# Product of the second expert table with its weights stationary, 32 tokens of it gathered instead, and the last gate computed with tokens along the free axis

## What is computed

```python
def peer(xn, w_pq, sub_k1, sub_k2, expert_u, expert_v):
    # 8 heads: top 16 of 128 keys on either side, top 16 of their 256 sums: 128 experts of 16384 a token
    act = jax.nn.gelu(jnp.einsum('tkd,td->tk', expert_u[ib], xb))
    return jnp.einsum('tk,tkd->td', act * gb, expert_v[ib])

h = h + peer(rms_norm_2(h, ffn_norm_gain), w_pq, sub_k1, sub_k2, expert_u, expert_v)
gate = jax.nn.sigmoid(rms_norm_2(h, ple_norm_gain) @ w_ple_gate)
h = h + gate * (p @ w_ple_proj)
```

## Time and profile before

| | us |
|---|---|
| median of 3 runs (3193.03 to 3201.77) | 3196.07 |
| the profiled execution, its own time | 3203.04 |
| its span | 3201.3 |
| PE busy | 3064.3 |
| DVE busy | 1886.7 |
| ACT busy | 1458.6 |
| granted clock of TensorE, mean share | 0.977 |

### The profile page before, as it was taken

One profiled execution on the slowest core, in us unless ns is written; L12 is line 12 of the kernel. 1 busy time (PEld: TensorE's weight loads), 2 busy tenths in 40 slices (PEclk: granted clock), 3 DMA queues, 4 the chain that ended last, 5 costly groups with the idle time before them and its releaser, 6 DMA issues. The chain is left out here.

```text
span 3201.3 us, 39991 instructions
## 1 busy us (share of the span) xinstructions
PE 3064.3 (96%) x15672; PEld 2653.1 (83%) x15672; DVE 1886.7 (59%) x2657; ACT 1458.6 (46%) x2137; POOL 159.9 (5%) x282
## 2 busy tenths in 40 slices
PE   8997689999998999999999999999999999999998
PEld 7996677888887887977789899889998888888876
DVE  4445355444444545464558987998755655655554
ACT  4333444444443444354444466347644444444443
POOL 2002100000000000140000100110000000000000
PEclk9996699999999999999999999999999999999999
DMA  7552045555554554545567888888787666777653
GB/s 247 188 188 68 0 148 172 192 185 194 185 188 158 192 196 145 173 142 178 192 211 247 281 304 305 293 278 294 257 276 241 240 231 242 242 248 248 216 194 131
DMA packets 219049, 665.24 MB, mean 208 GB/s; under 512 B 11705, under 2 KB 87513, under 8 KB 169488
## 3 DMA queue, kind: packets, MB, share of 16 engines
q1 hardware_dynamic: 208592, 607.36, 56.6%
q0 software_dynamic: 5440, 35.80, 3.2%
q10 hardware_dynamic: 4864, 19.99, 1.7%
HBM read 623.25 MB, written 37.77 MB: 206 GB/s over the span
## 5 line engine op out<-in xcount | busy, mean ns | idle before, releaser
L195 DVE TENSOR_TENSOR weights_lo<-weights,weights_hi 128x1024 fp32r<-128x1024 f32 (+4 forms) x1080 | 1227.5, 1178 | 974.8 <-ACT weights_hi L188 973.3
L188 ACT ACTIVATE weights_hi<-weights 128x1024 fp32r<-128x1024 f32 (+4 forms) x1080 | 1046.8, 1018 | 1508.8 <-PE banks L444 1121.4
L2185 PE MATMUL banks<-peer_features,weights_hi 128*128 128x448 f32 (+1 forms) x2304 | 743.7, 378 | 18.7 <-DVE weights_lo L195 18.6
L442 PE MATMUL banks<-weights_hi,features_hi 128*128 128x512 f32 (+3 forms) x1728 | 651.5, 377 | 11.4 <-DVE weights_lo L195 11.3
L444 PE MATMUL banks<-weights_hi,features_lo 128*128 128x512 f32 (+3 forms) x1728 | 649.3, 376 | 0.0
L443 PE MATMUL banks<-weights_lo,features_hi 128*128 128x512 f32 (+3 forms) x1728 | 649.1, 376 | 0.0
L2186 PE MATMUL banks<-peer_features,weights_lo 128*128 128x224 f32 (+1 forms) x2304 | 615.1, 267 | 0.0
L2185 PEld LDWEIGHTS banks<-peer_features,weights_hi 128*128 128x128 f32 x2304 | 431.9, 187 | 68.7 <-DVE weights_lo L195 27.9
L2186 PEld LDWEIGHTS banks<-peer_features,weights_lo 128*128 128x128 f32 x2304 | 438.6, 190 | 0.0
L442 PE MATMUL banks<-weights_hi,applied_hi 128*128 128x512 f32 x1024 | 398.5, 389 | 1.1 <-DVE peer_scores L2362 1.1
L444 PE MATMUL banks<-weights_hi,applied_lo 128*128 128x512 f32 x1024 | 398.4, 389 | 0.0
(11 more groups left out here) (377 smaller groups left out, 2101.8 us busy)
## 6 DMA issues: line engine op xcount, KB each, us to landing
weights<-in_expert_u SPq DMA_DIRECT2D x128, 1024.0 KB, 5.8
weights<-in_expert_v SPq DMA_DIRECT2D x128, 1024.0 KB, 5.0
weights<-in_w_ffn_gate SPq DMA_DIRECT2D x44, 1024.0 KB, 5.2
weights<-in_w_ffn_up SPq DMA_DIRECT2D x44, 1024.0 KB, 5.2
weights<-in_w_ffn_down SPq DMA_DIRECT2D x44, 1024.0 KB, 5.0
weights<-in_w_in SPq DMA_DIRECT2D x48, 900.0 KB, 4.7
weights<-in_w_out SPq DMA_DIRECT2D x32, 1024.0 KB, 5.2
weights<-in_w_in SPq DMA_DIRECT2D x24, 704.0 KB, 4.4
```

What stands on the lines that cost most here:

```text
L188: act.activation(hi[:, k, n], raw[:, k, n], ACT.Copy).then_inc(self.hi_ready, 1 + skip)
L195: last = dve.tensor_tensor(lo[:, k, n], raw[:, k, n], hi[:, k, n].bitcast(F32), ALU.subtract)
L442: pe.matmul(out, xh, wh, start=first, stop=False)
L2185: pe.matmul(self.bank(n % 3, 2 * (T - lo)), wh[:, k, :], F[:, k, :, lo:T], start=(k == 0), stop=False)
```

## The change

Five things are done.

1. **Table V turned.** The weights are stationary in chunks of 128 features, the gates of tokens 32 to 255 stream (224 columns): 16 chunks of three matmuls a piece. Of the three, the two with the rounded part of the weights come first (L2300, L2301), then lo weights (L2302). Two chunks share a bank; eight matmuls with a zero matrix (L2299) clear the banks first.
2. **V gathered for tokens 0 to 31.** POOL issues 32 more indirect DMAs, from the second table. DVE multiplies each with a weight and adds it to `row_sum`, in two halves (`ADD`, 64 instructions over steps 158 to 261). PE folds the sum in at e = 122 with 16 small matmuls (L2290). No one-hots and no stored scores for these tokens: buffers `S`, `a_hi`, `a_lo`, `s_in`, `g_in` lose 32 tokens.
3. **`SUM` moved.** The 64 half-row products of U stand at steps 56, 57, 58 to 73 and 108 to 153, one a step, none inside a retrieval step between 22 and 55 or 74 and 107.
4. **X transposed early.** At the eight steps 76, 79, ... 97 (`BACK`) PE transposes four blocks of X (L2263), and ACT copies them back, so that X has features on partitions.
5. **The gate continues the loop.** The pieces of w_ple_gate are steps 272 to 287 of the same block, weights stationary, 256 tokens streaming: 48 matmuls a piece. Adds, features, squares, and the result by groups of chunks are spread over the steps on ACT and DVE; the output is stored by features and turned on the host.

```diff
-        SC, RET, TURN = 18, (22, 74), (55, 107, 122)
-        HOT = [(58 + i, 0, ROWS // 8 + i) for i in range(16 - ROWS // 8)] + [(110 + i, 1, i) for i in range(16)]\
-            + [(126 + i, 0, i) for i in range(ROWS // 8)]
-        SUM = [34 + 4 * k // 3 for k in range(2 * ROWS)]
+        SC, RET, TURN = 18, (22, 74), (55, 107)
+        HOT = [(58 + i, 0, ROWS // 8 + i) for i in range(16 - ROWS // 8)] + [(110 + i, 1, i) for i in range(16)]
+        SUM = [56, 57, *range(58, 74), *range(108, 154)]
         DOTS = SUM[-1] + 1
+        free = [s for s in range(DOTS + 4, 262) if s % 8 != 2]
+        ADD = [free[k * len(free) // (2 * ROWS)] for k in range(2 * ROWS)]
+        GATHERED, BACK = NKEYS - 6, [76 + 3 * j for j in range(KD // 2)]
+        ROWSUM, SPREAD = 4, 6
...
-                    for c in range(ROWS):
+                    for c in range(2 * ROWS):
...
-                        pool.indirect_dma_start(out=rows[:, c % BUFS, :], out_offset=None, in_=rows_d,
-                                                in_offset=bass.IndirectOffsetOnAxis(ap=pick[:, c:c + 1], axis=0))\
+                        pool.indirect_dma_start(out=rows[:, c % BUFS, :], out_offset=None, in_=rows_d if c < ROWS else values_d,
+                                                in_offset=bass.IndirectOffsetOnAxis(ap=pick[:, c % ROWS:c % ROWS + 1], axis=0))\
...
-                        for t in ((1, 0) if e == 0 else (0, 1)):
-                            if e == 0 and t == 0:
-                                pe.wait_ge(tile_read, V0)
-                            for c in range(4):
-                                cols, tok = slice(c * BANK, (c + 1) * BANK), slice(t * P, (t + 1) * P)
-                                last = self.passes(pe, self.bank(4 * t + c), a_hi[:, q % 2, e % 2, tok], a_lo[:, q % 2, e % 2, tok],
-                                                   wh[:, cols], wl[:, cols], e == 0, e == NKEYS - 1)
+                        gh, gl = a_hi[:, q % 2, e % 2, :], a_lo[:, q % 2, e % 2, :]
+                        for c in (range(KD) if e > 0 else [*range(6, KD), *range(6)]):
+                            if e == 0 and c in (0, 2, 4):
+                                pe.wait_ge(tile_read, V0 - 2 + c // 2)
+                            out, cols = self.bank(c // 2, DENSE, c % 2 * T + ROWS), slice(c * P, (c + 1) * P)
+                            if e == 0 and c % 2 == 0:
+                                pe.matmul(self.bank(c // 2), zero[:, :], wh[:, 0:BANK], start=True, stop=False)
+                            pe.matmul(out, wh[:, cols], gh, start=False, stop=False)
+                            pe.matmul(out, wh[:, cols], gl, start=False, stop=False)
+                            last = pe.matmul(out, wl[:, cols], gh, start=False, stop=(e == NKEYS - 1 and c % 2 == 1))
...
+                    for s in range(KD):
+                        b, piece = s // 4, s % 4
+                        i, j, half = at(END + s)
+                        ring.wait(pe, i, j, half)
...
+                            for k in range(4):
+                                kk = 4 * piece + k
+                                if b == c == 0 and k % 2 == 0:
+                                    pe.wait_ge(*f_lo(kk // 2 + 1))
+                                out, cols = self.bank(4 * (b % 2) + c, T), slice(c * P, (c + 1) * P)
+                                pe.matmul(out, wh[:, k, cols], F[:, kk, 0, :], start=(kk == 0), stop=False)
+                                pe.matmul(out, wh[:, k, cols], F[:, kk, 1, :], start=False, stop=False)
+                                last = pe.matmul(out, wl[:, k, cols], F[:, kk, 0, :], start=False, stop=(kk == KD - 1))
...
+                            if c == 0:
+                                last = dve.tensor_scalar(to, row, weight, None, ALU.mult)
+                            else:
+                                last = dve.scalar_tensor_tensor(out=to, in0=row, scalar=weight, in1=to, op0=ALU.mult, op1=ALU.add)
...
+                    for s in range(KD):
+                        i, j, half = at(END + s)
+                        if s == 0:
+                            add(0)
+                            add(1)
...
+                        ring.split_lo(dve, ple_tiles, i, j, half)
+                        if s < 4:
+                            feature_lo(2 * s)
+                            feature_lo(2 * s + 1)
+                            if s < 3:
+                                add(2 * s + 2)
+                                add(2 * s + 3)
```

More of the change, by code:

```diff
@@ L1558, in project @@
             def project(pe, c, banks):
-                for t in range(NT):
+                for m in range(4):
                     for k in range(2):
-                        last = pe.matmul(self.bank(banks + t), pT[:, k, tok(t)], wproj[c // 2][:, c % 2, k, :],
-                                         start=(k == 0), stop=(k == 1))
+                        last = pe.matmul(self.bank(banks + m // 2, T, m % 2 * T), wproj[c // 2][:, c % 2, k, m * P:(m + 1) * P],
+                                         pT[:, k, :], start=(k == 0), stop=(k == 1))
                 last.then_inc(projected, 1)
@@ L2247, in _ @@
                                 last.then_inc(applied, 1)
                         last.then_inc(ring.used, 1)
+                    for s in range(KD):
+                        b, piece = s // 4, s % 4
+                        i, j, half = at(END + s)
+                        ring.wait(pe, i, j, half)
+                        wh, wl = [ring.piece(w, half, ple_tiles) for w in (ring.hi, ring.lo)]
+                        for c in range(4):
+                            if piece == 0 and b < 2:
+                                pe.wait_ge(added, 4 * b + c + 1)
+                            if piece == 0 and b >= 2:
+                                pe.wait_ge(gate_left, 2 * (b - 2) + c // 2 + 1)
+                            for k in range(4):
[6 more added lines that the diff above has]
+                                last = pe.matmul(out, wl[:, k, cols], F[:, kk, 0, :], start=False, stop=(kk == KD - 1))
+                            if b == 3 and piece == 3 and c < 3:
+                                last.then_inc(applied, 1)
+                        last.then_inc(ring.used, 1)
+                        if s == ROWSUM:
+                            pe.wait_ge(*x_squared(KD // 2 + 1))
+                            for t in range(NT):
+                                last = pe.matmul(self.bank(0, 1, T + t), total[:, 0, t * P:(t + 1) * P], self.ones[:, 0:1],
+                                                 start=True, stop=True)
+                            last.then_inc(self.squares.sem, 1)
+                        if s == SPREAD:
+                            pe.wait_ge(diag, 2)
+                            for t in range(NT):
+                                last = pe.matmul(self.bank(1, P, T + t * P), self.ones[:, :], diagonal[:, t * P:(t + 1) * P],
+                                                 start=True, stop=True)
+                            last.then_inc(spread, 1)
@@ L2400, in _ @@
                             dve.wait_ge(spread, 1)
-                            ch(dve.memset(S[:, :, :, 0:ROWS], 1.0))
+                            for quarter in range(4):
+                                ch(dve.tensor_copy(row_rstd[quarter * 32:quarter * 32 + 32, :], self.rstd[0:ROWS, 0:1]))
+                            dve.tensor_scalar(zero[:, :], self.ident[:, :], 0.0, None, ALU.mult)
+                            ch(dve.tensor_reduce(sel[:, :], self.ident[:, :].rearrange("p (q t) -> p t q", q=4), AX.X, ALU.add))
                         if s == 10:
@@ new lines, in feature_lo @@
+                    def feature_lo(j):
+                        dve.wait_ge(*f_hi(j + 1))
+                        for i in range(2):
+                            hi, lo = [f[:, 2 * j + i, :] for f in F_ple]
+                            last = dve.scalar_tensor_tensor(out=lo, in0=XT[:, j, i], scalar=ple_gains[2 * j + i],
+                                                            in1=hi.bitcast(F32), op0=ALU.mult, op1=ALU.subtract)
+                        last.then_inc(self.turned_read["dve"].sem, 1)
@@ L2463, in peer @@
+                    for n in range(6, len(groups)):
+                        scale(n)
+                        if n > 6:
+                            out(n - 1)
+                    out(len(groups) - 1)
             self.turn_split_close(gains)
```

334 lines of the change are left out of this document (214 added, 120 removed).

## The result

The changed kernel takes 3149.17 us (median of 4 runs, 3145.07 to 3151.32) against 3198.65 (4 runs): a ratio of 0.9846, 95% interval 0.9826 to 0.9865, so 49.5 us less. I had forecast 3130 with a range of 3095 to 3174. The direction and the range held; the gain is 49.5 us where my sum had 68.8. One sign that I had set myself did not hold: the second table was to be under 670 us, and it takes 692.8.

A forecast was written before the change was run, and what follows sets the result against it. PE was taken as busy nearly throughout, with DVE setting the pace in the first table's retrievals and two stretches without PE. The terms summed to -68.8 us, median 3127, stated as 3130 us, range 3095 to 3174.

The forecast's parts named there:

- Step 1: Second table: 6144 matmuls of 224 columns at 107 ns replace 3072 of 512, -39.0 us; added PE work +1.8 and +3.8.
- the first rival: Second table and gate: weight loads pace short matmuls, 113 ns apart, 37 and 5 us longer, total 3172; chance 0.15.
- the line: Matmul start distances, fitted through 512 and 352 columns: 0.419 ns a column and 12.2 ns beside them.
- Step 2: Second table: DVE's adds and POOL's gathers cost nothing, DVE's share going from 0.58 to about 0.76 under PE's cover.
- Step 3: First table's retrievals: half-row products moved out let pieces approach PE's 5.01 us, -23.0 us with a tenth left.
- Step 4: First table's one-hot steps: four go, each 1.85 us over a quiet piece, -7.4 us.
- Step 5: X turned early: 32 transposes of 0.12 us among PE's own work, +3.9 us; ACT's copies hidden.
- Step 6: Between second table and gate: the 10.2 us break goes but for 0.5 us, -9.7 us.
- Step 7: Gate: 768 matmuls of 256 columns replace 384 of 512, +5.9 us, or +10.5 with the pair's 126.5 ns.
- Step 8: Tail behind the last matmul: 14.3 us shrinks to 5.2, -9.1 us.
- Step 9: DMA in steps 126 to 153: gathers join weights, scores and gates at 337 to 350 GB/s, +4 us.
- DMA that can't follow: Gathers share engines with weights, scores and gates: at 290 GB/s +62 us, 3188; at 270 3243; chance 0.10.

The follow-up runs named there:

- e8_upair: Changed kernel with the first table's lo-weight matmul streaming 128 token columns instead of 224 in 14 of 16 chunks: 3144.82 us.
- e6_nogather: Changed kernel without the 32 gathers from the second table and DVE's waits for them, the adds kept: 3150.02 us.
- e5_sumback: Changed kernel with the first table's half-row products back at their old steps: 3168.81 us, ratio 0.9909 to the kernel before.
- e9_break: Changed kernel with all adds and features made in one block before the gate's first piece is split: 3156.50 us, ratio 0.9869 to the kernel before.
- e3_order: Changed kernel with the second table's three matmuls a chunk in the old order: 3151.19 us, ratio 0.9853 to the kernel before.
- e1_128: Changed kernel with the second table's matmuls streaming 128 token columns instead of 224: 3188.05 us, a single run.
- e2_half: Changed kernel with 64 of 128 stationary columns in the second table's matmuls, except in the first and last piece: 3095.75 us.
- e7_96x128: Changed kernel with 96 stationary columns and streams of 128 in the second table, except in the first and last piece: 3441.98 us, a single run.

## Why the prediction was right, and where it missed

- **Step 1, the distance in the second table, is the term that was mis-sized.** It had -39.0 for the matmuls alone; measured 6144 x 0.1117 = 686 against 696, -10. By my own signs, 0.112 and a second table of 670 us or more, the first rival is what happened. I had named this mechanism with 0.15 and nearly the right size, 113 ns, and set it aside by one argument: both pairs have 7 ns over the line, so the surcharge belongs to the pair. (Its 3172 was too high: it charged the gate 5 us that didn't come, and the other terms were better than my sum.) The argument doesn't hold. In the pair with 224 columns the load explains it (200 + 112 = 312, and e8_upair). For the pair with 256 it doesn't, since the gate's chain of 256 columns runs at the line's 120 ns; where those 7 ns come from stays open. The lower end, 0.10 us, was the distance between two starts, which is not the time that either takes. The chain of short matmuls that did stand in the trace, was the better witness. The formula that step 1 cites from the Trainium skill ("TensorE: Matmul & The Clock Gate", Back-to-back issue gap) is given there for a single matmul, not for a stream in which each brings its own weights.
- The zero products, +1.8: the first piece takes 7.21 us (2358.45 to 2365.66) against 5.36, +1.85. The fold-in, +3.8: its 32 records take 3.5 us, from 3014.22 to 3017.71. A term is missing behind it: the piece that follows takes 7.07 us instead of 5.36, +1.7, since the granted clock fell. In the window of the changed kernel right behind the fold-in PE is busy at 1.2 GHz:

```profile
3018.00:3021.00 3.00, 3.00 (x16) 3.00 (x15) 0.46 (x1) 0.00 (x0) 0.00 (x0) 0.50 0.65 208
```

- **Step 2**, gathers and adds in the second table hidden: right. DVE is busy 487 of 693 us, 0.70, where I had 0.76; e6_nogather shows no change.
- **Step 3**, -23.0: right, and the tenth that I left was not needed. 24 x 0.47 and 33 x 0.31 are 21.5 us with the transposes inside; without their 3.9 it is all of the 25.4. e5_sumback gives back 19.6 by the medians and 23.1 in the trace of the first table. The 23.1 with the transposes inside are 27 without them: pieces beside the 24 and 33 that I counted became faster too.
- **Step 4**, -7.4: the pieces from 126 to 129 lost their one-hots and went from 6.80 to 5.01 us, together 7.2. **Step 5**, +3.9: eight times four transposes; in pieces of 5.13 against 5.01 us it is 3.8.
- **Step 6**, -9.7, measured -10.1. e9_break shows that it is the order of DVE's work that does it.
- **Step 7**, +5.9, measured +6.3. The 256 columns are on the line.
- **Step 8**, -9.1, measured -9.8.
- **Step 9**, +4, measured 0: PE is never idle in the 80 us at 372 GB/s. I had taken 355 as the full rate from a share of 0.88; the trace goes beyond it.

The other rivals fell: the second of two matmuls with the same weights (e3_order), columns alone (e1_128), a stream on top of the load (0.112 is less than 0.18), retrievals that stay slow (5.01 us), and DMA that can't follow. No run points to a version that beats the changed kernel: 64 stationary columns free the stream but double the matmuls, and the rest of PE's time is full but for the 1.7 us that the clock costs behind the fold-in. A single matmul for both products with hi weights, writing twice to the same columns, wasn't tried on the chip.

## What to carry to other kernels

For fp32r matmuls that each bring their own 128 stationary columns, budget the larger of about 112 ns and the stream. By the line the two meet near 240 streamed columns (an estimate), and a shorter stream than that gains nothing. Look for a chain of short matmuls in the trace, however odd its line, before extrapolating from long ones, and read a chain by its period, never by one distance in a mixed pair. When several engines share steps, first ask whose queue sets the step: moving 64 products on DVE gave more here (about 20 us) than turning the matmuls of a 700 us stage (10). And look at the granted clock of a stage before you compare distances: at 1.2 GHz the same load took 213 ns.

## What the runs showed of the hardware

- The load of the stationary columns set the distance. At 2.4 GHz it was 111.7 ns for 128 columns whether 224 or 128 streamed, and 85 ns for 96. At 1.2 GHz it was 213 ns for 128 and 160 ns for 96. The Trainium skill ("TensorE: Matmul & The Clock Gate", LDWEIGHTS) gives columns / 1.2 in ns, 107 for 128 and 80 for 96; the traces agree within 5 ns at 2.4 GHz. At 1.2 GHz the runs show twice its figure.
- With 64 stationary columns a stream of 224 starts every 103 ns, 9.6 ns beside its columns at 2.4 GHz, where chains of 512 have 13.4.
- The granted clock fell to 1.2 GHz while PE was busy. In the changed kernel, e2_half, e5_sumback, e8_upair and e9_break it was 1.00 before the fold-in (32 records of 32 streamed columns), 0.50 for some us behind it, and 1.00 again while 224 columns streamed. In e3_order and e6_nogather the same 32 records left it at 1.00. What decides between the two stays open.
- With 128 stationary and 128 streamed columns behind the fold-in (e1_128) the clock stayed at 0.50 for 68 us, up to the gate. The same matmuls had held 1.00 for 660 us before the fold-in.
- With 96 stationary and 128 streamed columns (e7_96x128) it held 1.00 for the first 8 us. It was 0.50 soon after an idle time of 1.33 us, and for 968 us from then on, with PE busy, up to the gate. With under half the multiplications in the second table this kernel was 293 us slower than the changed one. No run has these matmuls without the idle time, so it isn't shown which of the two brought the fall.
- Behind 9.38 us without PE (e9_break) the clock was 0.50 for the next 4.5 us. In the kernel before, the 10.1 us between second table and gate, with PE busy for 4.7 of them, left it at 1.00.
